# A two-block transformer kernel: the last 128 columns of each unit's high weights 160 bytes further on, the value units' weights 128 bytes, and attention's output rows at the other rows' offset

## The reference, cut to what matters

```python
proj = jnp.einsum('btd,dn->btn', n, w_in[l])
merged = (jax.nn.sigmoid(gate_a) * jnp.einsum('btv,vd->btd', y_gdn, w_branch_gdn[l])
          + jax.nn.sigmoid(gate_b) * jnp.einsum('btv,vd->btd', y_dsa, w_branch_dsa[l]))
mix = jnp.einsum('btd,de->bte', merged, w_out[l])
u = jnp.square(jax.nn.relu(jnp.einsum('btd,df->btf', n2, w_up[l])))
h = h + _rmsnorm(jnp.einsum('btf,fd->btd', u, w_down[l]), post_mlp_norm[l])
...
y = jax.nn.sigmoid(ga) * (attn @ w_ao) + jax.nn.sigmoid(gf) * (four @ w_fo)
return y @ w_o
```

## Time and profile before

| | |
|---|---|
| time, median of three runs | 1173.78 us (1172.25 to 1173.88) |
| time of the profiled execution | 1169.99 us |
| its span, first to last instruction | 1168.2 us |
| granted TensorE clock, mean | 0.998 of full speed |
| busy share | PE 97%, DVE 57%, ACT 42% |
| split units prepared | 104: ACT 199.1 us, DVE 238.0 us in all |

### The profile page before, as it was taken

The page is one execution under the profiler, slowest core; times in us unless marked ns, Lnnn a source line. Parts: engine busy times, 40 slices in busy tenths (PEclk is TensorE's granted clock), DMA queues, the critical chain, the costliest instruction groups (busy, mean ns, idle before and its releaser), DMA issues.

```text
span 1168.2 us, 21501 instructions
## 1 busy us (share of the span) xinstructions
PE 1137.1 (97%) x8980; PEld 980.4 (84%) x8980; DVE 668.7 (57%) x1160; ACT 494.7 (42%) x777; POOL 84.7 (7%) x92
## 2 busy tenths in 40 slices
PE   9999999999999999999999999999999999999997
PEld 8998889998979989999979889767899866665664
DVE  7777966588776467775465342775656641221123
ACT  5775534635373655553535221667534311111112
POOL 2541320000000100000100000000001100000000
PEclk9999999999999999999999999999999999999999
DMA  9634330544415656555564322301956999999992
GB/s 368 226 144 181 109 146 1 176 150 144 181 38 181 254 219 251 184 208 186 190 244 190 114 93 73 145 2 62 355 213 256 379 418 423 424 426 424 424 427 90
DMA packets 36205, 254.61 MB, mean 218 GB/s; under 512 B 4048, under 2 KB 4192, under 8 KB 5904
## 3 DMA queue, kind: packets, MB, share of 16 engines
q1 hardware_dynamic: 33552, 237.84, 52.5%
q0 software_dynamic: 2560, 15.42, 3.3%
HBM read 252.19 MB, written 1.05 MB: 217 GB/s over the span
## 4 chain that ended last, share of the span: by engine, by line
PE 86%; DVE 9%; ACT 2%; issue 1%; DVEq 0%; ACTq 0%
PE bank L1427 15%; PE bank L727 12%; PE bank L721 12%; PE bank L722 12%; PE bank L1134 5%; PE bank L682 4%; PE bank L1220 4%; PE bank L1141 2%; PE bank L1439 2%; PE bank L1461 2%; PE bank L743 1%; PE bank L906 1%; DVE ring_low L2188 1%; PE bank L774 1%; PE bank L1246 1%
## 5 line engine op out<-in xcount | busy, mean ns | idle before, releaser
L2188 DVE TENSOR_TENSOR ring_low<-ring,w_high 128x2048 fp32r<-128x2048 f32 x104 | 238.0, 2290 | 148.8 <-ACT w_high L1698 148.8
L1698 ACT ACTIVATE w_high<-ring 128x2048 fp32r<-128x2048 f32 x104 | 199.1, 1916 | 279.0 <-PE bank L727 194.2
L721 PE MATMUL bank<-nT_high,w_high 128*128 128x256 f32 (+1 forms) x448 | 114.6, 296 | 0.0
L721 PEld LDWEIGHTS bank<-nT_high,w_high 128*128 128x128 f32 x448 | 84.5, 189 | 2.6 <-issue 2.4
L1427 PE MATMUL bank<-more,xs 128*64 128x256 f32 x768 | 84.5, 379 | 0.0
L1427 PEld LDWEIGHTS bank<-more,xs 128*64 128x64 f32 x768 | 55.0, 137 | 29.4 <-issue 2.3
L721 PE MATMUL bank<-hcl,w_high 128*128 128x256 f32 (+1 forms) x272 | 73.2, 306 | 0.0
L722 PE MATMUL bank<-hcl,w_high 128*128 128x256 f32 (+1 forms) x272 | 71.0, 298 | 0.0
L722 PE MATMUL bank<-nT_low,w_high 128*128 128x256 f32 (+1 forms) x272 | 64.6, 281 | 0.0
L721 PE MATMUL bank<-nMs,w_high 128*128 128x256 f32 x256 | 61.2, 284 | 0.0
L1134 PE MATMUL bank<-up,w_high 128*128 128x256 f32 x512 | 60.6, 276 | 0.0
(11 more groups left out here) (580 smaller groups left out, 2452.9 us busy)
## 6 DMA issues: line engine op xcount, KB each, us to landing
ring<-stream SPq DMA_DIRECT2D x163, 1024.0 KB, 5.1
more<-stream SPq DMA_DIRECT2D x60, 1024.0 KB, 18.9
more<-stream POOLq DMA_DIRECT2D x10, 1024.0 KB, 16.0
c<-constants_one SPq DMA_DIRECT2D x1, 1657.0 KB, 16.5
qc<-h_in SPq DMA_DIRECT2D x4, 272.0 KB, 3.5
c<-constants_two POOLq DMA_DIRECT2D x1, 1056.0 KB, 10.0
beside<-stream POOLq DMA_DIRECT2D x1, 1024.0 KB, 13.3
hT<-h_in POOLq DMA_DIRECT2D x1, 1024.0 KB, 6.0
```

The costliest lines, as they stand in the source:

```text
L721: nc.tensor.matmul(into[j], w, high_x(k), start=first, stop=False, skip_group_check=True)
L1698: A(w_high[:, d % 2, :], ring[:, s, :], ACT.Copy).then_inc(high_ready, 1)
L2188: TT(ring_low[:, s, :], ring[:, s, :], w_high[:, d % 2, :], sub).then_inc(low_ready, 1)
```

## The change

The last of the 16 blocks of a unit's high weights goes 40 words (160 bytes) further on in its buffer, which becomes 64 words longer. In the value units the whole of the high weights begins 32 words (128 bytes) further on. Where a unit's high weights now are in two pieces, ACT writes them with two instructions in place of one, and DVE's subtraction is likewise two; the semaphore is raised by the second. PE has the same 8980 products in the same order, with other addresses. A padding tensor of 32 words ahead of `y_dsa_low` goes away.

```diff
+HIGH_SLOT = KT * UNIT_COLS + 64
+LAST_BLOCK = KT * UNIT_COLS - 128
+LAST_SHIFT = 40
...
-        w_high = sbr(dense, "w_high", 128, 2, KT * UNIT_COLS)
+        w_high = sbr(dense, "w_high", 128, 2, HIGH_SLOT)
...
-                _before_y_dsa_low = sb(m, "before_y_dsa_low", 128, HALF_LINE)
                 y_dsa_low = sbr(m, "y_dsa_low", 128, H, SEQ)
...
+        def high_pieces(d):
+
+            if SPLIT_UNITS[d][0] == "v2":
+                return [(w_high[:, d % 2, HALF_LINE:HALF_LINE + KT * UNIT_COLS], slice(0, KT * UNIT_COLS))]
+            return [(w_high[:, d % 2, 0:LAST_BLOCK], slice(0, LAST_BLOCK)),
+                    (w_high[:, d % 2, LAST_BLOCK + LAST_SHIFT:LAST_BLOCK + LAST_SHIFT + 128], slice(LAST_BLOCK, KT * UNIT_COLS))]
+
+        def high_block(d, i):
+
+            at = 128 * i + (LAST_SHIFT if 128 * i == LAST_BLOCK else 0)
+            return w_high[:, d % 2, at:at + 128]
...
-                        w = high_w[:, k, j * 128:(j + 1) * 128]
+                        w = high_block(d, 2 * k + j)
...
-                    A(w_high[:, d % 2, :], ring[:, s, :], ACT.Copy).then_inc(high_ready, 1)
+                    for high, cols in high_pieces(d):
+                        ins = A(high, ring[:, s, cols], ACT.Copy)
+                    ins.then_inc(high_ready, 1)
...
-                    TT(ring_low[:, s, :], ring[:, s, :], w_high[:, d % 2, :], sub).then_inc(low_ready, 1)
+                    for high, cols in high_pieces(d):
+                        ins = TT(ring_low[:, s, cols], ring[:, s, cols], high, sub)
+                    ins.then_inc(low_ready, 1)
```

More of the change, by code:

```diff
@@ L703, in split_unit @@
                 pe.wait_ge(high_ready, d + 1)
-                return s, cnt, d, [w.rearrange("p (k n) -> p k n", n=cols) for w in (w_high[:, d % 2, :], ring_low[:, s, :])]
+                return s, cnt, d, ring_low[:, s, :].rearrange("p (k n) -> p k n", n=cols)
             def low_parts(d):
@@ L1127, in _ @@
                 for kg in range(4):
-                    s, cnt, d, (high_w, low_w) = split_unit("down", cp * 4 + kg)
+                    s, cnt, d, low_w = split_unit("down", cp * 4 + kg)
                     if cp == 0:
@@ L1133, in _ @@
                             for part in range(2):
-                                nc.tensor.matmul(dst[:, j * SEQ:(j + 1) * SEQ], high_w[:, k, j * 128:(j + 1) * 128], up[:, kg * KT + k, part, :],
+                                nc.tensor.matmul(dst[:, j * SEQ:(j + 1) * SEQ], high_block(d, 2 * k + j), up[:, kg * KT + k, part, :],
                                                  start=(kg == 0 and k == 0 and j == 0 and part == 0), stop=False, skip_group_check=True)
@@ L1151, in keys_of_context @@
                 pe.wait_ge(ctx_low_ready, 1)
-                s, cnt, d, (high_w, low_w) = split_unit("k2", 0)
+                s, cnt, d, low_w = split_unit("k2", 0)
                 dst = [take(("k2", j)) for j in range(2)]
-                keys_begun.append((s, cnt, high_w, low_w, dst))
+                keys_begun.append((s, cnt, d, low_w, dst))
                 for k in range(KT):
@@ L1157, in keys_of_context @@
                         for part in (2, 3):
-                            nc.tensor.matmul(dst[j][:, SEQ:2 * SEQ], high_w[:, k, j * 128:(j + 1) * 128], hcl[:, part, k, :],
+                            nc.tensor.matmul(dst[j][:, SEQ:2 * SEQ], high_block(d, 2 * k + j), hcl[:, part, k, :],
                                              start=(k == 0 and part == 2), stop=False, skip_group_check=True)
@@ L1166, in keys_of_stream @@
             def keys_of_stream():
-                s, cnt, high_w, low_w, dst = keys_begun[0]
+                s, cnt, d, low_w, dst = keys_begun[0]
                 for k in range(KT):
@@ L1172, in keys_of_stream @@
                         for part in (0, 1):
-                            nc.tensor.matmul(dst[j][:, 0:SEQ], high_w[:, k, j * 128:(j + 1) * 128], hcl[:, part, k, :],
+                            nc.tensor.matmul(dst[j][:, 0:SEQ], high_block(d, 2 * k + j), hcl[:, part, k, :],
                                              start=False, stop=False, skip_group_check=True)
@@ L1215, in _ @@
             for u in range(4):
-                s, cnt, d, (high_w, low_w) = split_unit("v2", u)
+                s, cnt, d, low_w = split_unit("v2", u)
+                high_w = high_pieces(d)[0][0].rearrange("p (k n) -> p k n", n=UNIT_COLS)
                 dst = [take(("v2", u, tp)) for tp in range(2)]
@@ L1314, in _ @@
                         mod_unit(22 + u)
-                s, cnt, d, (high_w, low_w) = split_unit("fo", half, 512)
+                s, cnt, d, low_w = split_unit("fo", half, 512)
+                high_w = lambda i: high_block(d, i)
+                low_of = lambda i: low_w[:, i // 4, 128 * (i % 4):128 * (i % 4) + 128]
                 if half == 0:
@@ L1320, in four_by_weights @@
                 def four_by_weights(u, j, k, x, w, first=False, last=False):
-                    a = u * 256 + j * 128
-                    return nc.tensor.matmul(dst[u][:, j * SEQ:(j + 1) * SEQ], w[:, k, a:a + 128], x[:, k, :], start=first, stop=last, skip_group_check=True)
+                    return nc.tensor.matmul(dst[u][:, j * SEQ:(j + 1) * SEQ], w(4 * k + 2 * u + j), x[:, k, :], start=first, stop=last, skip_group_check=True)
                 for u in range(2):
@@ L1332, in _ @@
                         for k in range(4):
-                            last = four_by_weights(u, j, k, four_high, low_w, last=(k == 3))
+                            last = four_by_weights(u, j, k, four_high, low_of, last=(k == 3))
                     if u == 0:
```

4 lines of the change are left out of this document (2 added, 2 removed).

## The result

The change makes the kernel slower: 1175.38 us, the median of 13 runs (1173.12 to 1177.19), against 1170.56 us of the kernel before over 13 runs (1168.58 to 1173.88). The ratio is 1.004, with a 95% interval from 1.003 to 1.0049. The three runs of before on which the prediction was made (median 1173.78 us) lay high in that spread, by 3.2 us. So 4.0 us less were forecast and 4.8 us more came.

The account below looks back on a forecast made before the run. PE's products times the distance between their starts, plus a few stops, were taken to bound the kernel. The terms 0.7 - 1.8 - 1.8 - 1.1 = -4.0 us, on the median 1173.78, gave 1169.8 us; 8-in-10 range 1167 to 1176.5.

Parts of the forecast that it names:

- What bounds the kernel: On PE: time is nearly products times distance between starts, 113.3 ns (close) or 117.8 ns (wide), chosen anew at stops.
- I take that the jump ends a wide run where it occurs: At each unit's displaced last block: low products become close, -1.8 us, and units following without a stop, -1.8 us.
- The sign that I had named for it: In the MLP, 454 to 598 us: low rows turning to 1.88 us would show the prediction wrong in sign.
- the jump throws close runs out of step: At the last block, close low parts and followers turn wide: 3.3 + 5.6 + 0.7 us, 1177.8 to 1183.4 us; chance 0.16.
- Its point of decision: Across all units: the sign turns as soon as close units thrown out exceed wide units freed.
- Two instructions in place of one: Split copies on ACT and subtractions on DVE: 0.11 and 0.08 us each on the chain, +0.7 us, bounds 0 and 1.4.
- Value units: High weights 128 bytes on: the high part's 256 products become close, -1.1 us; low part stays wide; bounds 0 and 1.7.
- Attention's output rows at 160: In the four `bd` units: nothing counted in addition, bounds 0 and 0.9 us.
- Nothing moves: Everywhere: runs keep the distance their stops chose, leaving 0.7 us; 1174.5 us, between 1173.1 and 1175.8; chance 0.27.

Follow-up runs that it names:

- The kernel with six loads: The change with the last three blocks of a unit 160 bytes further on in place of one: 1179.42 us, ratio 1.0078.
- two blocks: The change with the last two blocks of a unit (four loads) 160 bytes further on in place of one: 1170.2 us, ratio 0.9992.
- the first trial: The change with only ten units split, their last two blocks 160 bytes further on, and all other units whole: 1167.98 us, ratio 0.9976.
- the kernel without displacement: The change without the last block's shift and without the split; value units and attention's rows as in the change: 1167.96 us, ratio 0.9972.
- the last of the two trials: The change with the first eleven units whole and every later unit's last block 128 bytes further on: 1168.34 us, ratio 0.998.

## Why the prediction was wrong

*What bounds the kernel* held: the time is the number of products times the distance of their starts, the distance is kept from unit to unit, and the two distances are some 113.3 and 117.8 ns in every kernel here.

*The step that failed* is "I take that the jump ends a wide run where it occurs", with its -1.8 and -1.8 us. I had asked of the displaced block only what it does to a wide run, and that it does: of 40 units that come in wide 39 go out close (356.88 us). I took no account of the same block in a close run. There it does the opposite, as the rows 451.19 and 456.65 us show, and before had more close units than wide ones. The term was not -3.6 us but +3.6 us by the products of the two traces; against kernels that differ in the displacement alone it is 5 to 6 us. The sign that I had named for it came: rows of the MLP turned to 1.89. That 1175.38 us lies inside the stated range, up to 1176.5, is luck: the range was laid around a time of before that was 3.2 us too high, and as a difference it ended at +2.7 us.

*The rival "the jump throws close runs out of step"* had the mechanism. Its price was too high (+8.9 us and the split) because it let the wide runs stay as they were; in fact about half of each kind of unit changes places. The kernel with six loads, 1179.42 us, is what that rival describes. Its point of decision was right: slower as soon as the close units thrown out exceed the wide ones that are freed.

*Two instructions in place of one*: 0.7 us, measured as a ratio of 1.0009 with an interval that holds it and zero, while the products of that trace take 1.4 us less than in before. That 0.7 fits is luck. A split by itself was sized nearly right (0.07 and 0.09 us for 0.08 and 0.11), but one piece, behind GpSimd at 24.28 us, cost 0.65 us, which no term of the sum had.

*Value units*: forecast -1.1 us, measured -1.06, all of it in the high part, and the low part stays wide, as I had it. The reason that I gave does not hold, though: the first unit of `f2`, whose close distance behind the same rotation I had carried over, comes in wide in all eleven kernels with the value units at their new start, and close in the three without. And in four of the eleven (two blocks, the first trial, 32 and 64 bytes) the first value unit kept the wide distance. So the number is right in part by luck: here too a stop chooses.

*Attention's output rows at 160*: I counted nothing, with a bound of 0.9 us. In the trace of the kernel without displacement the whole run of `bd` and `gate_b` units is close, 1.5 us. Of the three kernels with these rows at 32 the first unit behind that stop begins wide in all three; of the eleven with rows at 160, close in ten. So the row offset bears on the distance that the stop leaves, though one jump inside a run moves a single start. I had missed that a row offset can count at a run's beginning while it does not count within it.

*"Nothing moves"* fell: between 128 and 160 bytes for one block's loads, with everything else equal, lie 7 us in the medians and two patterns of starts. The rule that was weighed, from the Trainium skill, "TensorE: Matmul & The Clock Gate", section "Step-by-step: what each phase is for", says that loading the next weights takes no read bandwidth of SBUF from the running product. The trace does not bear out what I drew from it, that no address can change a distance; whether it is read bandwidth that is lost, or something else between the load and the rows, the traces don't show.

*What stays open.* I found no rule by which the displacement (32, 64, 128, 160, 256 bytes) or the number of loads decides whether distances are kept, ended or exchanged. Which distance a stop leaves is open too. Nor is it shown why the units' products, which take 2.5 us less in the last of the two trials than in the kernel without displacement (3.6 against 1.1 us less than in before), leave no trace in the medians (1168.34 against 1167.96 us). The split may take some of it. The lower clock does not hide the rest: at a mean granted clock of 0.998 the two kernels took 1166.31 to 1167.05 and 1166.35 to 1167.11 us, at 0.995 1168.85 to 1169.01 and 1168.66 to 1169.6 us. Nor is the clock all that differs between executions: those of before at 0.995 go from 1169.2 to 1173.4 us. Each kernel has one trace, so it is not known whether its runs begin wide or close in the same places in every execution.

## What to carry to other kernels

When an edit is meant to push products out of a slow steady pattern, count first the products that are already in the good one, and price what the edit does to them: the same disturbance meets both. Try such an edit alone and in two or three sizes, since here the size decided between 0.998 and 1.004. Ship the parts that need no further instruction first: different starts for whole tensors gave 0.28% by themselves. An instruction that is cut in two can let another engine's waiting instruction in between, and a piece of 0.28 us then took 0.86 us.

## What the runs showed of the hardware

Products of 256 columns with loads of 128 have two steady distances, 113.3 and 117.8 ns (16 low products in 1.81 or 1.89 us), that outlast changes of rows, ring slot and bank. Two loads at another start can keep them, end the wide one or exchange the two, by the size of the displacement as in the table.

A subtraction on VectorE (ring less `w_high`) and a TENSOR_TENSOR on GpSimd held each other up here: of 100 second pieces the 13 that began while GpSimd's was in flight ended 0.15 us behind it and took 0.83 to 0.87 us in place of 0.28; GpSimd's, begun inside DVE's first piece, took 2.16 us at 24.90 us in place of 0.77.

TensorE's granted clock falls in some executions at places where others, with the same work there, keep it. One row of PE's timeline of the changed kernel (these 16 matmuls took 2.05 us in the change without its split in the first units):

```profile
184.53 3.56 PE L976 MATMUL bank<-metas,scr 128*128 128x128 f32 x16 [0.37 <-ACT metas L1696]
```

That is the lower level, 1.2 GHz, behind a part with many small products of 64 columns and short waits; the granted clock is 0.85 from 182 to 186 us and 0.72 from 186 to 190 us. Of the 14 kernels' profiled executions eight have it there; two with the split in the first units have it not, and one without that split has it. It costs some 1.5 us, a third of the effect that this study was about, and twelve runs of one kernel spread over 2.6 to 5.7 us.
